# Experts in strict big/small alternation, and down-projection weights as 8 KB rows, in a weight-streaming encoder kernel

## The reference, cut to what matters

```python
def moe(h, router, w_gate_up, w_down):
    xt = h.reshape(B * S, D)                       # 256 x 1024
    probs = jax.nn.softmax(xt @ router)            # 8 experts
    top_p, top_i = lax.top_k(probs, 2)
    ...
    for e in range(8):                             # w_gate_up[e] 1024 x 5632, w_down[e] 2816 x 1024
        y = y + gates[:, e:e + 1] * swiglu(xt, w_gate_up[e], w_down[e])
```

## Time and profile before

| | |
|---|---|
| median of three runs | 1169.89 us |
| profiled execution: its own time | 1167.88 us |
| profiled execution: span, first to last instruction | 1166.0 us |
| mean granted TensorE clock | 0.979 |
| PE busy | 93% of the span |
| DVE, ACT busy | 54%, 45% |
| traffic of SP's queue | 341.94 MB, mean of all DMA 295 GB/s |

### The profile page before, as it was taken

How to read it: one execution, slowest core, us unless ns; L and a number is a source line. 1 busy time by engine, 2 the same in 40 slices (tenths; PEclk the granted TensorE clock), 3 DMA queues, 4 the chain that set the end, 5 groups by cost and what they waited for, 6 DMA issues and landing times.

```text
span 1166.0 us, 15739 instructions
## 1 busy us (share of the span) xinstructions
PE 1089.2 (93%) x5708; PEld 800.3 (69%) x5708; DVE 625.4 (54%) x693; ACT 522.0 (45%) x571; POOL 22.5 (2%) x93
## 2 busy tenths in 40 slices
PE   7899999999999988999999999999998999999774
PEld 7867788888898777787446786446787788443131
DVE  6755555555654448895108894008886997301002
ACT  5544544344445644773016773016775676110001
POOL 2100000000000000000000000000000000000000
PEclk9889999999999999999999999999999999999998
DMA  9932455555454424997999999999999999799995
GB/s 353 335 108 86 165 184 184 177 186 211 145 182 147 140 73 146 370 361 270 379 409 409 400 410 396 391 409 410 400 409 367 343 361 357 287 403 409 406 403 202
DMA packets 122455, 343.47 MB, mean 295 GB/s; under 512 B 12893, under 2 KB 39562, under 8 KB 122378
## 3 DMA queue, kind: packets, MB, share of 16 engines
q1 hardware_dynamic: 122234, 341.94, 78.5%
q10 hardware_dynamic: 144, 0.52, 0.1%
HBM read 341.37 MB, written 1.05 MB: 294 GB/s over the span
## 4 chain that ended last, share of the span: by engine, by line
PE 75%; SPq 9%; DVE 5%; DMA 4%; issue 3%; ACT 3%; POOL 0%; POOLq 0%; DVEq 0%; ACTq 0%
PE ps L1454 19%; PE ps L1455 19%; PE ps L1456 19%; PE ps L1459 16%; SPq L361 5%; SPq L365 4%; DMA raw<-moe_w_gate_up_dram 3%; ACT whi L547 1%; DMA raw<-moe_w_down_dram 1%; DVE wlo L948 1%; PE ps L1789 1%; PE ps L1469 1%; DVE h L1131 1%; DVE wlo L937 0%; ACT xs L547 0%
## 5 line engine op out<-in xcount | busy, mean ns | idle before, releaser
L547 ACT ACTIVATE whi<-raw 128x2048 fp32r<-128x2048 f32 (+1 forms) x195 | 335.8, 1725 | 241.2 <-PE ps L1456 231.2
L948 DVE TENSOR_TENSOR wlo<-raw,whi 128x2048 fp32r<-128x2048 f32 x151 | 345.8, 2293 | 123.1 <-ACT whi L547 121.3
L1454 PE MATMUL ps<-whi,xhi 128*128 128x512 f32 (+3 forms) x688 | 265.7, 386 | 13.9 <-DVE wlo L948 5.1
L1455 PE MATMUL ps<-whi,xlo 128*128 128x512 f32 (+3 forms) x688 | 261.7, 380 | 0.0
L1456 PE MATMUL ps<-wlo,xhi 128*128 128x512 f32 (+3 forms) x688 | 261.3, 380 | 0.0
L1459 PE MATMUL ps<-raw,xs 128*64 128x512 f32 (+2 forms) x1024 | 158.5, 462 | 10.5 <-DMA raw<-moe_w_gate_up_dram 10.4
L1454 PEld LDWEIGHTS ps<-whi,xhi 128*128 128x128 f32 x688 | 131.1, 190 | 41.9 <-DVE wlo L948 7.4
L1456 PEld LDWEIGHTS ps<-wlo,xhi 128*128 128x128 f32 x688 | 130.9, 190 | 24.2
L1455 PEld LDWEIGHTS ps<-whi,xlo 128*128 128x128 f32 x688 | 130.9, 190 | 22.5
L1459 PEld LDWEIGHTS ps<-raw,xs 128*64 128x64 f32 x1024 | 67.1, 137 | 98.2 <-issue 65.6
L1454 PE MATMUL ps<-whi,hhi 128*128 128x512 f32 x264 | 106.5, 403 | 0.0
(11 more groups left out here) (282 smaller groups left out, 973.9 us busy)
## 6 DMA issues: line engine op xcount, KB each, us to landing
raw<-moe_w_gate_up_dram SPq DMA_DIRECT2D x256, 512.0 KB, 12.2
raw<-moe_w_down_dram SPq DMA_DIRECT2D x176, 512.0 KB, 14.0
raw<-moe_w_gate_up_dram SPq DMA_DIRECT2D x96, 384.0 KB, 9.5
raw<-ffn_w_gate_up_dram SPq DMA_DIRECT2D x44, 512.0 KB, 4.9
raw<-ffn_w_down_dram SPq DMA_DIRECT2D x22, 512.0 KB, 4.0
raw<-kv_shared_w_dram SPq DMA_DIRECT2D x16, 512.0 KB, 3.7
raw<-moe_w_gate_up_dram SPq DMA_DIRECT2D x32, 256.0 KB, 9.8
raw<-mla_w_o_dram SPq DMA_DIRECT2D x8, 512.0 KB, 14.0
```

Source lines behind the costliest of these rows:

```text
L547: return nc.scalar.activation(o, i, ACT.Copy, scale=scale)
L948: V.tensor_tensor(wlo[:, s, :].rearrange("p a w -> p (a w)"), raw[:, (hh // 2) % RAW, :], whi[:, s, :].bitcast(F32).rearrange("p a w -> p ...
L1454: pe.matmul(o, a_hi, b_hi, start=start, stop=False, skip_group_check=True)
L1455: pe.matmul(o, a_lo, b_hi, start=False, stop=False, skip_group_check=True)
```

## The change

Two things are changed at once.

1. **Order.** The items run big, small, big, small to the end. Table rows are laid out as pairs, the loop on every engine goes over pairs, and the trip count is in pairs. Overflow items now also come in pairs of one big and one small slot size; DVE has to give each overflowing expert a row of its size, which takes more tiny instructions in the routing. Buffers, the code of an item, the units and their slots are the same.
2. **Down units.** Units 22 to 31 become one transfer each of 1 MB: partition p receives rows 2p and 2p+1 of the 256 rows, 8 KB that lie together in memory, where before it received row p and row 128+p in two transfers. The last unit (32) stays as it was. As the down rows are now dealt out alternately, the transposes take every second column of `gu` (a stride of 8 bytes) in place of 128 neighbours.

```diff
-ORDER = (0, 1, 5, 2, 6, 7) + OVF * (-1,) + (3, 4)
+ORDER = (0, 1, 5, 2, 6, 3, 7, 4) + OVF * (-1,)
 def transfers(x):
-    return len(segments(x)) if x < GU else 2
+    return len(segments(x)) if x < GU else 1 if x < FU - 1 else 2
+def interleaved(t, j):
+    w = t.shape[1]
+    if j == SUB - 1:
+        return [t[:, b * P:(b + 1) * P] for b in range(w // P)]
+    v = t.rearrange("p (u q n) -> p u n q", n=2, q=P)
+    return [v[:, b // 2, b % 2, :] for b in range(w // P)]
...
+                elif x < FU - 1:
+                    of = w_dn[(x - GU) * 256:(x - GU + 1) * 256, :].rearrange("(p n) d -> p (n d)", n=2)
+                    sp_eng.dma_start(raw[:, u % RAW, :], of).then_inc(landed[u % RAW], 16)
...
-            final = act.value_load(final_i[0:1, 0:1], min_val=NB - 1, max_val=NB - 1 + OVF)
-            with act.Fori(PAIRS, final) as i:
-                big(i, i + PAIRS, "big")
-            big(final, final + PAIRS, "small")
-            small(PAIRS, final + PAIRS + 1, "small")
-            small(PAIRS + 1, final + PAIRS + 2, None)
+            final = act.value_load(final_i[0:1, 0:1], min_val=PAIRS - 1, max_val=PAIRS - 1 + OVF // 2)
+            with act.Fori(PAIRS - 2, final) as p:
+                big(p, 2 * p, "small")
+                small(p, 2 * p + 1, "big")
+            big(final, 2 * final, "small")
+            small(final, 2 * final + 1, None)
...
-            V.tensor_scalar(cap[:, :], place[:, :], 0.5, float(SMALL), ALU.is_gt, ALU.mult)
-            step(V.tensor_scalar(cap2[:, :], place[:, :], NS + 0.5, float(SMALL), ALU.is_gt, ALU.mult))
-            step(V.tensor_tensor(cap[:, :], cap[:, :], cap2[:, :], ALU.subtract))
-            step(V.tensor_scalar(cap[:, :], cap[:, :], -float(P), None, ALU.add))
+            V.tensor_scalar(cap2[:, :], place[:, :], 0.5, None, ALU.is_gt)
+            step(V.tensor_scalar(wide[:, :], place[:, :], NS + 0.5, None, ALU.is_gt))
...
-                    for b in range(w // P):
-                        last = pe.transpose(ps[:, TR_BANK, b * P:(b + 1) * P], gm[:, j % 2, b * P:(b + 1) * P], ident[:, :])
+                    for b, block in enumerate(interleaved(gm[:, j % 2, 0:w], j)):
+                        last = pe.transpose(ps[:, TR_BANK, b * P:(b + 1) * P], block, ident[:, :])
```

More of the change, by code:

```diff
@@ L55 @@
 NS = 4
[L56 to L61, removed]
-ORDER = (0, 1, 5, 2, 6, 7) + OVF * (-1,) + (3, 4)
+PAIRS = N_EXP - NS
+OVF = 6
+FIRST_OVF = 2 * PAIRS
+ITEMS = FIRST_OVF + OVF
+ORDER = (0, 1, 5, 2, 6, 3, 7, 4) + OVF * (-1,)
 SUB = 6
@@ L208, in build @@
             ("sp", [P, HEADS, 384], F32))
-        lg, lg2, oh1, oh2, sc8, msk, gates, posn, posc, ovf, csum, key, place, cap, cap2, less, order, oh, prod, \
+        lg, lg2, oh1, oh2, sc8, msk, gates, posn, posc, ovf, csum, key, place, cap, cap2, wide, csum2, extra, less, order, oh, prod, \
             m1, m2, den, best, rank, cnt, tf, xr = over(
@@ L213, in build @@
                   ("lg", "lg2", "oh1", "oh2", "sc8", "msk", "gates", "posn", "posc")],
-                *[(f"rt_{n}", [P, N_EXP], F32) for n in ("ovf", "csum", "key", "place", "cap", "cap2")],
+                *[(f"rt_{n}", [P, N_EXP], F32) for n in ("ovf", "csum", "key", "place", "cap", "cap2", "wide", "csum2", "extra")],
                 ("rt_less", [P, N_EXP, N_EXP], F32), ("rt_order", [P, ITEMS], F32),
@@ L442, in _ @@
             sp_eng.wait_ge(items_ready, 2)
-            for p in range(PAIRS):
+            for p in range(PAIRS - 2):
                 small_loads(p, at(2 * p + 1), lambda x: after_big(x, p))
                 big_loads(p + 1, at(2 * p + 2), lambda x: after_small(x, p))
[L446 to L450, removed]
+            final = sp_eng.value_load(final_i[0:1, 0:1], min_val=PAIRS - 1, max_val=PAIRS - 1 + OVF // 2)
+            with sp_eng.Fori(PAIRS - 2, final) as p:
+                small_loads(p, at(2 * p + 1), lambda x: after_big(x, p))
+                big_loads(p + 1, at(2 * p + 2), lambda x: after_small(x, p))
+            small_loads(final, at(2 * final + 1), lambda x: after_big(x, final))
             for c in range(TC):
@@ L530, in _ @@
             pool.wait_ge(items_ready, 2)
-            final = pool.value_load(final_i[0:1, 0:1], min_val=NB - 1, max_val=NB - 1 + OVF)
-            with pool.Fori(0, final + NS) as g:
-                scatter_weights(g + 1)
+            final = pool.value_load(final_i[0:1, 0:1], min_val=PAIRS - 1, max_val=PAIRS - 1 + OVF // 2)
+            with pool.Fori(1, 2 * final + 2) as g:
+                scatter_weights(g)
             norm(4)
@@ L1176, in gathered_low, with item_gates, choose @@
                                                op0=ALU.mult, op1=ALU.subtract).then_inc(xe_lo, 1)
[L1178 removed]
+            def item_gates(g):
                 dve.wait_ge(h_ready[4], g * 4 + 4)
[L1180 to L1184 removed]
+                V.tensor_copy(gt[:, :], g_tab[:, bass.ds(g, 1), :].rearrange("p a c -> p (a c)")).then_inc(gt_ready, 1)
+            def choose(g, following):
+                V.tensor_copy(pm[:, :, :], pm_tab[:, bass.ds(g, 1), :, :].rearrange("p a b c -> p (a b) c")).then_inc(pm_ready, 1)
                 dve.wait_ge(pm_ready, g)
@@ L1204, in add_in, with big @@
                                                op0=ALU.mult, op1=ALU.add).then_inc(h_ready[4], 1)
-            def big(i, g, row, following, next_row):
+            def big(i, g, following):
                 def gate(j):
@@ L1226, in big @@
                     if x == 14:
-                        item_gates(g, row)
-                        choose(g + 1, next_row, following)
+                        item_gates(g)
+                        choose(g + 1, following)
                     if x == FU - 1:
@@ L1243, in big, with small @@
                 add_in(g)
-            def small(p, g, row, following, next_row):
+            def small(p, g, following):
                 def gate(j):
@@ L1394, in _ @@
+            step(V.tensor_scalar(wide[:, :], place[:, :], NS + 0.5, None, ALU.is_gt))
+            step(V.tensor_tensor(wide[:, :], cap2[:, :], wide[:, :], ALU.is_equal))
+            step(V.tensor_scalar(cap[:, :], wide[:, :], -float(P - SMALL), -float(SMALL), ALU.mult, ALU.add))
             step(V.tensor_tensor(ovf[:, :], cnt[:, :], cap[:, :], ALU.add))
             step(V.tensor_scalar(ovf[:, :], ovf[:, :], 0.0, None, ALU.is_gt))
-            step(V.tensor_tensor_scan(csum[:, :], ones[:, 0:N_EXP], ovf[:, :], 0.0, ALU.mult, ALU.add))
+            step(V.tensor_tensor(wide[:, :], wide[:, :], ovf[:, :], ALU.mult))
@@ new lines, in _ @@
+            step(V.tensor_tensor(cap2[:, :], ovf[:, :], wide[:, :], ALU.subtract))
+            V.tensor_tensor_scan(csum[:, :], ones[:, 0:N_EXP], wide[:, :], 0.0, ALU.mult, ALU.add)
+            step(V.tensor_tensor_scan(csum2[:, :], ones[:, 0:N_EXP], cap2[:, :], 0.0, ALU.mult, ALU.add))
+            n_wide, n_narrow = csum[:, N_EXP - 1:N_EXP], csum2[:, N_EXP - 1:N_EXP]
+            V.tensor_scalar(extra[:, 0:1], n_wide, 1.0, None, ALU.min)
+            V.tensor_scalar(extra[:, 1:2], n_narrow, 0.5, None, ALU.is_gt)
@@ new lines, in _ @@
+            step(V.tensor_scalar(extra[:, 2:3], n_narrow, 2.5, None, ALU.is_gt))
+            step(V.tensor_tensor(extra[:, 1:2], extra[:, 1:2], extra[:, 2:3], ALU.add))
+            V.tensor_tensor(extra[:, 1:2], extra[:, 1:2], n_wide, ALU.max)
+            step(V.scalar_tensor_tensor(out=cap2[:, :], in0=csum2[:, :], scalar=extra[:, 0:1], in1=csum2[:, :],
+                                        op0=ALU.mult, op1=ALU.add))
+            V.scalar_tensor_tensor(out=extra[:, 2:3], in0=n_narrow, scalar=extra[:, 0:1], in1=extra[:, 1:2],
+                                   op0=ALU.mult, op1=ALU.max)
@@ L1404, in _ @@
             V.tensor_copy(item_expert[:, :], tf[:, :]).then_inc(items_ready, 1)
[L1405 removed]
+            V.tensor_scalar(final_i[:, :], extra[:, 2:3], float(PAIRS - 1), None, ALU.add).then_inc(items_ready, 1)
             gathered_low(0)
@@ L1427, in _ @@
                 split_low_unit(H_MOE + 2 * x)
-            for p in range(PAIRS):
-                big(p, 2 * p, 2 * p, "small", 2 * p + 1)
-                small(p, 2 * p + 1, 2 * p + 1, "big", 2 * p + 2)
+            for p in range(PAIRS - 2):
+                big(p, 2 * p, "small")
+                small(p, 2 * p + 1, "big")
             dve.wait_ge(items_ready, 2)
[L1432 to L1438, removed]
+            final = dve.value_load(final_i[0:1, 0:1], min_val=PAIRS - 1, max_val=PAIRS - 1 + OVF // 2)
+            with dve.Fori(PAIRS - 2, final) as p:
+                big(p, 2 * p, "small")
+                small(p, 2 * p + 1, "big")
+            big(final, 2 * final, "small")
+            small(final, 2 * final + 1, None)
+            n_items = 2 * final + 2
             dve.wait_ge(gbc_in, 16)
@@ L1831, in transposes @@
                         pe.wait_ge(hT_ready, p * SMALL_GROUPS + j)
-                    for b in range(SMALL_WIDTH[j] // P):
```

(9 more changed lines are left out.)

11 lines of the change are left out of this document (7 added, 4 removed).

## The result

The changed kernel takes 1150.0 us (median of four runs, 1148.64 to 1150.65), the kernel before 1169.74 in four runs. The ratio is 0.9829, with a 95% interval of 0.9812 to 0.9846: 20 us faster. The forecast was 1149.0 in a range of 1144 to 1156. The profiled execution took 1148.64 us, with a span of 1146.9; 1147.0 and 1145.1 were forecast for it.

What follows compares the result with a forecast made beforehand. The weight stream was taken as the bound, held back by full slots behind two big items. Span 1166.0 - 18.1 (order) - 3.2 (rows) + 0 (transposes) + 0.4 (routing) = 1145.1 us; against the median 1149.0, range 1144 to 1156.

Steps and rivals of the forecast that it cites:

- the order: In g4 to g7, two pairs like g2, g3 replace 362.50 us with 344.38 us: gain 18.1 us.
- the count of lost DMA time: Check on the order: 23.6 us lost in the 331 GB/s stretch, less 1.8 us per new pair: net 20.0 us.
- Rows of 8 KB: Down units take 0.08 us less each, counted in small items g1, g3, g5, g7: 3.2 us; bounds 0 and 5.6.
- The rate worked out from the two kinds of stretch: Row cost fitted from 409 and 393 GB/s stretches: 8 KB rows take 310.5 ns, a down unit 2.48 us, about 420 GB/s.
- Strided transposes: PE's transpose weight loads stay at 138 ns, cost 0; if loads take twice as long, 14.3 us over 104 loads.
- Routing: On DVE ahead of g0: 2.0 us of added instructions, 1.8 covered by waits for ACT, plus 0.15: about +0.4 us.
- One sign: Sign expected in the profile after: the first `xlo` on DVE is about 0.2 us later.
- Rows that bring nothing: Rival: 8 KB rows in down units gain nothing, since something beyond row cost sets the pace: 1152.2 us; 18%.
- rows that count everywhere: Rival: 8 KB rows count in big items too, or slots fill less: 1146.6 us, down to 1144.7; 12%.
- a slow load that reaches the time: Rival: strided weight loads at the transposes take twice the time, 14.3 us more: 1163.3 us; 7%.
- a single transfer that is slower: Rival: single large down transfers run slower than two of 4 KB rows; at 331 GB/s, 42 us more, 1194 us; 3%.
- an order that loses its gain elsewhere: Rival: lost DMA time reappears elsewhere, as the same volume goes through the same 11 slots: 1167.1 us; 4%.

Runs made afterwards that it cites:

- the order alone: Changed kernel's alternating order, with down units loaded as before (two transfers, 4 KB rows) and transposes of neighbouring columns: 1153.39 us, ratio 0.9861 to the kernel before.
- The moved pair of big items: Order-only kernel with items written out, run big, small, big, big, small, small, big, small: 1170.7 us, ratio 1.0002; 18.9 us over the written-out alternating control.
- the missing slot: Changed kernel with SP waiting in the items for the unit 10 places ahead instead of 11: 1161.85 us, ratio 0.9933 to the kernel before.
- the kernel with rows and plain transposes: Changed kernel with transposes of 128 neighbouring columns, so hidden features meet the wrong down rows: 1149.84 us, ratio 0.9827 to the kernel before.
- the order with strided transposes: Order-only kernel (4 KB rows) with strided transposes added, hidden features again out of step: 1152.44 us, ratio 0.9851 to the kernel before.
- order, items written out: Order-only kernel with all eight items written out in place of the loops, without overflow items: 1151.8 us, ratio 0.9846 to the kernel before.

## Why the prediction was right

**What bounds the kernel, and the order (forecast -18.1 us).** The step was to take a pair that stands in the old trace, 173.47 us, and to put it twice in place of what ran there. The pairs came out at 171.95 and 173.25 us, and the order alone gave 16.3 us (14.5 to 18.0) with the loops and 18.0 (15.2 to 20.7) without, both with the new routing in them. The moved pair of big items (18.9 us) and the missing slot (3 us a pair) show the mechanism. Of the two ways to work it out, the measured pair was nearer than the count of lost DMA time, 20.0 us. One step was off: the last pair was taken as a middle pair less one unit, 2.56 us. Over the seven traces of the alternating order with all 11 slots (table below) it is only about 1.3 us shorter than the middle pairs. That is most of why the profiled span came out at 1146.9 us, 1.8 over the forecast. A likely reason is that the stream runs thin at its end: in the changed kernel 413 GB/s over the 16 us ahead of g6, 352 over the 16 us up to the last unit. That is argued, not tested.

```profile
944.00:960.00 16.00, 15.46 (x86) 7.03 (x82) 2.67 (x9) 2.89 (x10) 0.00 (x0) 1.00 1.02 413
1115.50:1131.50 16.00, 11.95 (x54) 2.95 (x52) 0.00 (x0) 0.00 (x0) 0.00 (x0) 1.00 0.86 352
```

**Rows of 8 KB (forecast -3.2 us, bounds 0 and 5.6).** The rate worked out from the two kinds of stretch, 422 GB/s, is measured as 421. The gain: between the order alone and the kernel with rows and plain transposes, 0.9861 - 0.9827 is 4.0 us of 1170.9, with intervals of about 2 us to either side on each; from the order with strided transposes (0.9851) it is 2.8 us. "Down units of a big item only make the slots full sooner, nothing gained" is borne out by the run that leaves them out. The edit halves the number of rows and the number of transfers of a down unit at once, and no run separates the two, so the gain is that of rows of 8 KB in one transfer.

How the gain falls on the pairs is best read from several traces. First units of g2, g4, g6 and the last of g7, with the order alone:

```profile
615.91 1.91 ACT L558 ACTIVATE whi<-raw 128x2048 fp32r<-128x2048 f32 x1 [3.45 <-DMA raw<-moe_w_gate_up_dram]
...
788.92 1.91 ACT L558 ACTIVATE whi<-raw 128x2048 fp32r<-128x2048 f32 x1 [3.59 <-DMA raw<-moe_w_gate_up_dram]
...
962.10 1.91 ACT L558 ACTIVATE whi<-raw 128x2048 fp32r<-128x2048 f32 x1 [4.05 <-DMA raw<-moe_w_gate_up_dram]
...
1134.75 1.94 PE L1486 MATMUL ps<-raw,hT 128*64 128x512 f32 x8 [0.55 <-DMA raw<-moe_w_down_dram]
```

And with the rows and plain transposes:

```profile
614.18 1.91 ACT L558 ACTIVATE whi<-raw 128x2048 fp32r<-128x2048 f32 x1 [3.30 <-DMA raw<-moe_w_gate_up_dram]
...
786.85 1.91 ACT L558 ACTIVATE whi<-raw 128x2048 fp32r<-128x2048 f32 x1 [3.30 <-DMA raw<-moe_w_gate_up_dram]
...
959.77 1.91 ACT L558 ACTIVATE whi<-raw 128x2048 fp32r<-128x2048 f32 x1 [3.38 <-DMA raw<-moe_w_gate_up_dram]
...
1130.67 1.94 PE L1486 MATMUL ps<-raw,hT 128*64 128x512 f32 x8 [0.53 <-DMA raw<-moe_w_down_dram]
```

The same instructions in all seven traces of the alternating order with 11 slots, in us:

| run | down rows in small items | first unit of g2 | g2, g3 | g4, g5 | g6, g7 to the last unit | span |
|---|---|---|---|---|---|---|
| order alone | 4 KB | 615.91 | 173.01 | 173.18 | 172.65 | 1150.2 |
| order, strided transposes | 4 KB | 615.52 | 173.47 | 173.40 | 171.89 | 1149.7 |
| order, items written out | 4 KB | 615.84 | 173.16 | 173.76 | 171.74 | 1150.1 |
| changed kernel | 8 KB | 614.58 | 171.95 | 173.25 | 171.65 | 1146.9 |
| changed kernel, again | 8 KB | 614.34 | 172.70 | 173.09 | 171.62 | 1147.2 |
| changed, plain transposes | 8 KB | 614.18 | 172.67 | 172.92 | 170.90 | 1146.1 |
| changed, 8 KB rows in small items only | 8 KB | 614.66 | 172.57 | 172.92 | 171.37 | 1147.0 |

The mean span falls from 1150.0 to 1146.8 us, 3.2 us as forecast, and every column takes part: 1.3 us ahead of g2, then 0.7, 0.4 and 0.7. Even shares of 0.8 were forecast. The same pair of the same kernel differs by 0.75 us between two executions (171.95 and 172.70), so the traces neither show the even shares nor speak against them.

**Strided transposes (forecast 0, bound +14.3 us).** Right in the time, wrong in the reason. It was taken as free "since only the place of elements in a partition changes", with the load at 138 ns; it is 50% longer, 207 ns. It lies for the most part over other work of PE, since four transposes advance PE by 0.47 us in place of 0.44, and by 0.68 in place of 0.59 in a small item. By the advance, 22 x 0.0085 = 0.2 us a big item, and 0.1 for the first four of a small one, an estimate of about 1.1 us over four pairs. Neither run that takes the stride away or adds it shows a cost, and neither could show one so small. The bound of 14.3 us took each load as fully in PE's way, which none of these traces bears out. By the note on cachelines under "Door 1: The DMA port swizzle" on the page SBUF — State Buffer of the Trainium skill, a stride of two float32 is within what runs at full speed; the measured 207 ns against 138 differ from it, and the measurement decides.

**Routing (forecast +0.4 us).** Its 20 instructions are there, and the two waits for ACT before `xlo` are gone as the cover. The first changed instruction, the first `xlo`, the unit behind it and the first unit split behind the tables, in the profile after:

```profile
439.54 0.17 DVE L1401 TENSOR_SCALAR rt_cap<-rt_place 128x8 f32<-128x8 f32 x1
...
444.45 2.15 DVE L1185 SCALAR_TENSOR_TENSOR xlo<-ps,gcol,xhi 128x128 fp32r<-128x128 f32 x8
446.52 1.22 DVE L946 TENSOR_TENSOR wlo<-raw,whi 128x1024 fp32r<-128x1024 f32 x1
...
453.85 6.69 DVE L959 TENSOR_TENSOR wlo<-raw,whi 128x2048 fp32r<-128x2048 f32 x3
```

And in the one before, the last of them:

```profile
453.66 6.70 DVE L948 TENSOR_TENSOR wlo<-raw,whi 128x2048 fp32r<-128x2048 f32 x3 [0.38 <-issue]
```

That is +0.2 us, but DVE came to line 1401 already 0.35 us later than to line 1390 before (439.54 and 439.19). From there to the split it is 14.31 us after and 14.47 before. So the longer routing shows no cost; 0.4 us was a small term set too high. One sign was wrong: the first `xlo` is 1.2 us later (444.45 against 443.24), not 0.2, and the time comes back because the second four no longer wait.

**The rivals.** Rows that bring nothing, rows that count everywhere, a slow load that reaches the time, a single transfer that is slower, and an order that loses its gain elsewhere: none came. Of the two that differ from the forecast by 2 to 3 us, the median of 1150.0 alone would not decide; the runs with 4 KB rows and the one with 8 KB rows in small items only do.

## What to carry to other kernels

Where one stage consumes slower than its weights arrive and the next faster, what one step can lend the next is the free slots: alternate the two kinds rather than grouping them, and look at the rate of the stream over stretches of one step, not at the busy share of the engine. A pair of steps that already stands in the trace in the wanted order is a better price than a sum over its parts. A faster transfer is worth something only in steps that wait for it, and here one slot less cost 12 us, three to four times what all the larger rows bring.

## What the hardware showed beyond expectation

The granted clock of TensorE falls for a short stretch at the start of some big items, after PE has waited for the first unit, and in which ones differs from execution to execution. In the order-only kernel it fell at the start of g2 and of g6 but not of g4 (clock in the third column from the end; the last row is the fall at g2 itself, nearly all of it at half the full clock, which is the lower level, 1.2 GHz):

```profile
616.00:636.00 20.00, 17.72 (x69) 13.40 (x70) 17.29 (x12) 13.33 (x7) 2.15 (x1) 0.91 1.03 409
789.00:809.00 20.00, 16.13 (x69) 12.17 (x70) 16.95 (x12) 13.34 (x7) 2.29 (x1) 1.00 1.03 409
962.00:982.00 20.00, 17.45 (x68) 13.21 (x69) 16.69 (x11) 13.41 (x7) 2.75 (x1) 0.91 1.03 409
...
621.50:625.00 3.50, 3.50 (x10) 2.71 (x9) 3.29 (x2) 1.76 (x2) 0.00 (x0) 0.53 1.03 408
```

The fall is free, and the traces show why. Without it, PE waits once more some 14 us behind the first unit, for DVE's `wlo`; with it, PE comes to the same place in time with no wait. The order-only kernel at g2 (with the fall) and at g4 (without):

```profile
630.23 0.50 PE L1481 MATMUL ps<-whi,xhi 128*128 128x512 f32 x1
...
803.31 0.49 PE L1481 MATMUL ps<-whi,xhi 128*128 128x512 f32 x1 [1.57 <-DVE wlo L959]
```

These matmuls start 14.32 and 14.39 us behind the first unit of their item (615.91 and 788.92). The eleven traces of this study hold 30 big items behind a starved small one. In 9 of them the clock fell, and none of these has the second wait; the other 21 all have it, 1.4 to 1.6 us long. During the fall at g2 matmuls are spaced 0.43 us in place of 0.23, an estimate of 1.6 us for the eight of them, as much as the wait. So the slower clock takes the time that PE would have waited. The pairs agree: g2/g3 with the fall took 173.01 us and g4/g5 without it 173.18.
